# Strassen pairs of column blocks in the last FFN's second matrix, an eighth Strassen block in its first two, and six adaLN sums moved into FoX's head steps

## The reference

```python
for i in range(DEPTH):                       # DEPTH = 2
    mod = c_act @ ada_w[i] + ada_b[i]
    sh_a, sc_a, g_a, sh_f, sc_f, g_f = [m[:, None, :] for m in jnp.split(mod, 6, axis=-1)]
    h = x * (1.0 + sc_a) + sh_a
    y = _mla(h, ...) if i % 2 == 0 else _fox(h, ...)
    x = _layer_norm(ALPHA * x + (1.0 + g_a) * y, ln1_g[i], ln1_b[i])
    h = x * (1.0 + sc_f) + sh_f
    y = (silu(h @ w1) * (h @ w3)) @ w2
    x = _layer_norm(ALPHA * x + (1.0 + g_f) * y, ln2_g[i], ln2_b[i])
```

## Time and profile before

| | |
|---|---|
| median of 3 runs | 2184.3 us (2183.52 to 2187.05) |
| profiled execution | 2183.23 us |
| its span, first to last instruction | 2181.5 us |
| mean granted TensorE clock | 0.997 |
| busy | PE 98%, DVE 77%, ACT 47%, POOL 5% |

### The profile page before, as it was taken

How to read it: one execution, slowest core, us unless ns; L and a number is a source line. 1 busy time by engine, 2 the same in 40 slices (tenths; PEclk the granted TensorE clock), 3 DMA queues, 4 the chain that set the end, 5 groups by cost and what they waited for, 6 DMA issues and landing times.

```text
span 2181.5 us, 25010 instructions
## 1 busy us (share of the span) xinstructions
PE 2130.8 (98%) x9515; PEld 1737.1 (80%) x9515; DVE 1677.3 (77%) x1868; ACT 1024.9 (47%) x1334; POOL 105.1 (5%) x208
## 2 busy tenths in 40 slices
PE   5799999999999999999999999999999999999999
PEld 2378877888888888888788888878888888888887
DVE  6789989787777777778887566878787755787766
ACT  1077636544443444443544454554445534465543
POOL 2101100000000000000000000000000000000000
PEclk9999999999999999999999999999999999999999
DMA  9999997789998898999678778958985765576672
GB/s 388 418 363 365 360 391 271 283 296 336 338 338 328 322 337 323 325 332 366 216 270 329 258 270 288 343 178 267 348 301 206 277 230 175 162 257 217 223 281 85
DMA packets 177065, 635.90 MB, mean 291 GB/s; under 512 B 20385, under 2 KB 51377, under 8 KB 150705
## 3 DMA queue, kind: packets, MB, share of 16 engines
q1 hardware_dynamic: 147298, 427.93, 54.6%
q0 software_dynamic: 27792, 201.34, 24.7%
q10 hardware_dynamic: 1856, 5.04, 0.6%
HBM read 616.37 MB, written 17.86 MB: 291 GB/s over the span
## 4 chain that ended last, share of the span: by engine, by line
PE 87%; DVE 6%; DMA 5%; ACT 1%; issue 1%; POOL 0%; ACTq 0%; SPq 0%; DVEq 0%; POOLq 0%
PE ps L2106 45%; PE ps L2112 22%; PE ps L2409 7%; PE ps L2415 3%; PE ps L2123 3%; DMA gate<-in_ada_w 3%; PE ps L2391 2%; DMA raw<-in_mla_w_o 1%; DVE wlo L1356 1%; PE ps L2396 1%; DMA ada_head<-in_ada_w 1%; DVE ada_w L1393 1%; DVE gate L1393 1%; DMA ada_w<-in_ada_w 1%; PE ps L2335 0%
## 5 line engine op out<-in xcount | busy, mean ns | idle before, releaser
L850 ACT ACTIVATE whi<-raw 128x1024 fp32r<-128x1024 f32 (+1 forms) x645 | 679.0, 1056 | 852.6 <-PE ps L2112 698.4
L1356 DVE TENSOR_TENSOR wlo<-raw,whi 128x1024 fp32r<-128x1024 f32 (+1 forms) x645 | 777.2, 1214 | 356.2 <-ACT whi L850 354.2
L2106 PE MATMUL ps<-whi,hT_hi 128*128 128x512 f32 x1432 | 447.8, 394 | 2.3 <-DVE hT_lo L1784 2.3
L2106 PE MATMUL ps<-whi,hT_lo 128*128 128x512 f32 x1432 | 441.7, 390 | 0.0
L2112 PE MATMUL ps<-wlo,hT_hi 128*128 128x512 f32 x1432 | 382.9, 389 | 0.0
L1393 DVE CUSTOM_DVE_ANT_0 ada_w<-ada_w,c_bc,cols 128x2048 f32<-128x2048 f32 x145 | 339.7, 2344 | 14.8 <-ACT c_bc L1224 8.5
L2106 PEld LDWEIGHTS ps<-whi,hT_lo 128*128 128x128 f32 x1432 | 268.8, 188 | 56.6
L2112 PEld LDWEIGHTS ps<-wlo,hT_hi 128*128 128x128 f32 x1432 | 268.8, 188 | 56.2
L2106 PEld LDWEIGHTS ps<-whi,hT_hi 128*128 128x128 f32 x1432 | 266.1, 188 | 56.1 <-DVE hT_lo L1784 2.9
L2106 PE MATMUL ps<-whi,uT_lo 128*128 128x512 f32 x656 | 201.9, 389 | 0.0
L2106 PE MATMUL ps<-whi,uT_hi 128*128 128x512 f32 x656 | 201.9, 389 | 0.0
(11 more groups left out here) (317 smaller groups left out, 2028.9 us busy)
## 6 DMA issues: line engine op xcount, KB each, us to landing
raw<-in_ffn_w SPq DMA_DIRECT2D x436, 512.0 KB, 5.6
ada_w<-in_ada_w POOLq DMA_DIRECT2D x145, 1024.0 KB, 8.1
raw<-in_fox_w_in SPq DMA_DIRECT2D x96, 512.0 KB, 5.3
raw_more<-in_ffn_w SPq DMA_DIRECT2D x92, 512.0 KB, 5.3
ada_head<-in_ada_w POOLq DMA_DIRECT2D x16, 1024.0 KB, 20.1
raw<-in_mla_w_o SPq DMA_DIRECT2D x32, 512.0 KB, 8.7
raw<-in_fox_w_o SPq DMA_DIRECT2D x32, 512.0 KB, 5.4
gate<-in_ada_w POOLq DMA_DIRECT2D x12, 1024.0 KB, 8.9
```

The costliest lines, as they stand in the source:

```text
L850: nc.scalar.activation(split_hi(pl.unit)[:, 0:n], raw_of(pl.unit)[:, 0:n], ACT.Copy).then_inc(hi_ready, 1)
L1356: nc.vector.tensor_tensor(split_lo(pl.unit)[:, 0:n], raw_of(pl.unit)[:, 0:n], split_hi(pl.unit)[:, 0:n].bitcast(F32), ALU.subtract).then_i ...
L2106: nc.tensor.matmul(ps[:, 2 * pair + t, 0:width], a[:, t * P:(t + 1) * P], w_hi, start=(first and c == 0 and a is hi), stop=False)
```

## The change

Three things:

- `FAST_FROM` goes from 4 to 3: block 3 of the last FFN becomes a Strassen block too, the mixtures are made one block earlier, in block 2.
- In the last FFN's `w2`, pairs of column blocks become Strassen products (`FAST_PAIRS`): both pairs of the first pass and the first pair of the second. Of a pair's 24 (20) units four are replaced by seven operand units of 6 matmuls. The left-hand mixtures are made once per pass from `uT` (`pair_mix_inputs`, `pair_mix_low`, one ACT copy); per pair there are four operand sums, four ACT copies, two corrections, and for each side an addition to the banks' content, the gate's multiplication and the addition to x (`add_pair_side`), which take the place of `residual`.
- Layer 1's last 16 sums need no longer wait for the FFN: `one_ada` names the even steps, and the bound is the end of the list. Six sums leave the last FFN for the second place of FoX's steps 0, 4, 8, 12, 16 and 18.

```diff
-FAST_FROM = 4
+FAST_FROM = 3
...
+FAST_PAIRS = (2, 1)
+PAIR_LEFT, PAIR_RIGHT = (4, 0, 4), (6, 6, 6)
+
+
+def pair_units(n):
+
+    count = 4 * FF_PASSES[n] // UC
+    left, right = ([(side, j) for j in range(2, count)] for side in ("left", "right"))
+    return (left[:-2] + [("B11", 0), ("B21", 1)] + left[-2:] + right[:1] + [("B22", 1), ("T1", 0)]
+            + right[1:3] + [("T2", 0)] + right[3:5] + [("T3", 0)] + right[5:7] + [("T4", 0)] + right[7:])
...
-    return i % 4 == 2 and i < H
+    return i % 2 == 0
...
+    pair_left = [silu_all, place_at("pair_left_1", [P, T, NB], F32, b0 + 20 * KB)]
+    pair_right = [u, place_at("pair_right_1", [P, T, NB], F32, b0 + 44 * KB)]
...
+            def load_pair(n, first, pair, at):
+
+                for kind, j in PAIR_UNITS[n]:
+                    if kind in ONTO:
+                        pl.unit += 1
+                        at += 1
+                        continue
+                    load_down(1, n, first, 2 * pair + (kind in ("right", "B22")), j, at)
+                    at += 1
+                    if kind == "B21":
+                        s, free, _ = BESIDE[pl.unit - 1]
+                        sp.wait_ge(lo_ready, free)
+                        sp.dma_start(raw_tile(s), A["ffn_w2"][1, (2 * pair + 1) * (D_FF // P // UC) + 4 * first // UC]
+                                     ).then_inc(raw_in[s], 16)
+                return at
...
+                if i == FF_PASSES[0]:
+                    act.wait_ge(pair_added, 2 * FAST_PAIRS[0])
...
+            def fast_pair(n, pair, done):
+
+                q, at = n * FAST_PAIRS[0] + pair, PAIR_AT[n]
+                left, right = pair_left[n], pair_right[n]
+                if pair == 0:
+                    units(MIX_AT)
+                    act.wait_ge(mix_summed, 2 + n)
+                    nc.scalar.activation(pair_s_hi[n][:, :, :, :], pair_s_32[n][:, :, :, :], ACT.Copy
+                                         ).then_inc(mix_high, 1)
+                    done += MIX_AT
+                units(at["B11"] + 2 - done)
+                act.wait_ge(units_used, pl.pe - 2)
+                act.wait_ge(pair_added, 2 * q)
+                nc.scalar.activation(left[:, 0, :], ps[:, CHAIN, :], ACT.Copy).then_inc(pair_first_copied, 1)
+                units(at["T1"] + 1 - at["B11"] - 2)
+                act.wait_ge(units_used, pl.pe - 1)
...
-                    if layer == 0 or pl.ada < ada_end(1, SH_F):
+                    if layer == 0 or pl.ada < len(ADA_ORDER):
...
-                    if layer == 0 and i < TICKS - 1 and i not in (0, 2, 4) or layer == 1 and one_ada(i) and pl.ada < ada_end(1, SH_F):
+                    if layer == 0 and i < TICKS - 1 and i not in (0, 2, 4) or layer == 1 and one_ada(i) and pl.ada < len(ADA_ORDER):
...
+            def pair_mix_inputs(n):
+
+                dve.wait_ge(u_low_ready, U_BLOCKS + n * FF_PASSES[0] + 1)
+                dve.wait_ge(units_used, pl.pe)
+                chain(nc.vector.tensor_tensor(pair_mix32[n][:, :, :], uT_hi[:, 0:2 * UC, :].bitcast(F32),
+                                              uT_lo[:, 0:2 * UC, :].bitcast(F32), ALU.add))
+                (a11, a21), (a12, a22) = ([pair_mix32[n][:, x * UC:(x + 1) * UC, t * P:(t + 1) * P]
+                                           for t in range(T)] for x in range(2))
+                s = [pair_s_32[n][:, k, :, :] for k in range(4)]
+                mark(nc.vector.tensor_tensor(s[S1], a21, a22, ALU.subtract))
+                mark(nc.vector.tensor_tensor(s[S3], a11, a21, ALU.subtract))
+                own()
+                chain(nc.vector.tensor_tensor(s[S2], s[S1], a11, ALU.subtract))
+                nc.vector.tensor_tensor(s[S4], s[S2], a12, ALU.add).then_inc(mix_summed, 1)
+
+            def pair_mix_low(n):
+
+                dve.wait_ge(mix_high, 2 + n)
+                nc.vector.tensor_tensor(pair_s_lo[n][:, :, :, :], pair_s_32[n][:, :, :, :],
+                                        pair_s_hi[n][:, :, :, :].bitcast(F32), ALU.subtract).then_inc(mix_ready, 1)
+
+            def add_pair_side(side, bank, read, q, col, last, added):
+
+                dve.wait_ge(units_used, pl.pe)
+                own()
+                nc.vector.tensor_tensor(side[:, :, :], side[:, :, :], ps[:, bank:bank + T, :], ALU.add
+                                        ).then_inc(read, 1)
+                dve.wait_ge(gate_copied, 16 * pl.gate)
+                dve.wait_ge(read, q + 1)
+                for t in range(T):
+                    mark(nc.vector.tensor_tensor(side[:, t, :], side[:, t, :],
+                                                 gate[:, col * NB:(col + 1) * NB], ALU.mult))
+                own()
+                x = xa[:, :, col * NB:(col + 1) * NB]
+                nc.vector.tensor_tensor(x, x, side[:, :, :], ALU.add).then_inc(pair_added, 1)
+                if last:
+                    dve.wait_ge(pair_added, added)
+                    for t in range(T):
+                        mark(nc.vector.bn_stats(stats[:, t, col * 6:(col + 1) * 6],
+                                                xa[:, t, col * NB:(col + 1) * NB]))
+
+            def fast_pair(n, pair, done):
+
+                q, at = n * FAST_PAIRS[0] + pair, PAIR_AT[n]
+                left, right = pair_left[n], pair_right[n]
+                last = n == len(FF_PASSES) - 1
+                if pair == 0:
+                    units(1)
+                    pair_mix_inputs(n)
+                    units(MIX_AT)
+                    pair_mix_low(n)
+                    done += 1 + MIX_AT
+                units(at["T3"] + 1 - done)
+                dve.wait_ge(pair_fifth_copied, q + 1)
+                dve.wait_ge(pair_second_copied, q + 1)
+                dve.wait_ge(pair_third_copied, q + 1)
+                mark(nc.vector.tensor_tensor(right[:, 0, :], right[:, 1, :], right[:, 0, :], ALU.subtract))
+                mark(nc.vector.tensor_tensor(right[:, 1, :], right[:, 1, :], left[:, 1, :], ALU.subtract))
+                units(at["T4"] - at["T3"] - 1)
+                add_pair_side(left, PAIR_LEFT[q], pair_left_read, q, 2 * pair, last, 2 * q + 1)
+                units(len(PAIR_UNITS[n]) - at["T4"])
+                add_pair_side(right, PAIR_RIGHT[q], pair_right_read, q, 2 * pair + 1, last, 2 * q + 2)
...
+                for kind, j in PAIR_UNITS[n]:
+                    if (kind, j) == ("left", 2) and pair == 0:
+                        pe.wait_ge(u_low_ready, made - 1)
+                    if (kind, j) == ("left", count - 2) and pair == 0:
+                        pe.wait_ge(u_low_ready, made)
+                    if (kind, j) == ("left", 2) and pair == 0 and n == 1:
+                        pe.wait_ge(pair_left_read, q)
+                    if (kind, j) == ("right", 2):
+                        pe.wait_ge(right_read, done)
+                        if q:
+                            pe.wait_ge(pair_right_read, q)
+                    if kind == "B11":
+                        if q:
+                            pe.wait_ge(pair_third_copied, q)
+                        operand(CHAIN, rows_of_u(0, 0), True, True)
+                    if kind == "T1":
+                        if q:
+                            pe.wait_ge(pair_fifth_copied, q)
+                        operand(FIFTH, mixed_u(S1), True, True)
+                    if kind == "T2":
+                        pe.wait_ge(pair_first_copied, q + 1)
+                        operand(CHAIN, mixed_u(S2), False, True, True)
+                    if kind == "T3":
+                        pe.wait_ge(pair_second_copied, q + 1)
+                        operand(CHAIN, mixed_u(S3), False, True, True)
+                    if kind == "B21":
+                        operand(left, rows_of_u(1, 0), False, False)
+                    if kind == "T4":
+                        operand(left + 1, rows_of_u(1, 1), False, True)
+                    if kind == "B22":
+                        pe.wait_ge(mix_ready, 2 + n)
+                        operand(right, mixed_u(S4), False, False)
+                    if kind == "left":
+                        plain(left, j, j == 2, (j == count - 1, False))
+                    if kind == "right":
+                        plain(right, j, j == 2, (j == count - 1, j == count - 1))
...
```

141 lines of the change are left out of this document (114 added, 27 removed).

## The result

The changed kernel takes 2189.8 us (median of 20 runs, 2186.2 to 2192.7), the kernel before 2185.2 us (20 runs beside it). The ratio is 1.0019 with an interval of 1.0013 to 1.0025: about 4 us slower (the medians are 4.6 us apart), just inside what I had called no change, and 0.2 us above my range. I had started from 2184.3 us, the median of 3 runs of the kernel before; 20 runs put it at 2185.2, so 0.9 us of the distance to my 2184.2 is the starting point, and the rest is the change.

The account below looks back on a forecast made before the run. PE was taken as the bound, busy 2130.8 of 2181.5 us. Removed matmuls (-5.4) plus a stall in FoX's last steps (+5.3) gave -0.1 us, forecast 2184.2 us, 8-in-10 range 2178.6 to 2189.6.

Parts of the forecast that it names:

- what the change takes away: Last FFN: 24 fewer matmuls on PE at 0.227 us each, 5.4 us saved, with nothing overlapping.
- block 3 and the pairs cost nothing off PE: Last FFN: the added DVE and ACT work makes PE wait nowhere; priced at nothing.
- the pairs are not free: Rival, last FFN: PE waits 1 to 2 us in each of three pairs, time 2187 to 2190 us; 7%.
- the place: FoX's last steps: PE waits for the low half near 1403 to 1412 us, DVE's sums for DMA in steps 17 and 18.
- the stall doesn't come: Rival, FoX's last steps: loads are quick, PE loses less than 1 us, time 2178.9 us; 20%.
- the size of the stall: FoX's last steps: PE stands still for 5.3 us, with bounds of 1.7 and 8.1 us.
- With 7.3: the sum of step 17 can start at 1399.0.: FoX's last steps: with the median load time of 7.3 us, step 17's sum starts at 1399.0 and ends at 1401.3.
- My upper bound: FoX's last steps: with loads of 8.7 us the low half ends at 1414.4, a stall of 8.1 us.
- Where I began to follow the buffers: FoX's step 16, with times of the earlier trace; its added sum's data, issued at 1384.34, arrive at most 8.7 us later.
- In two pieces of 0.9 and 4.4.: Stall split: 0.9 us at P times V of head 15, 4.4 at the unit needing head 15's low half.
- The lower bound, 1.7: FoX's last steps: with loads of 5.0 us only the sums are in the way, leaving 1.7 us of stall.
- The rival of the clock: Rival, FoX's last steps: PE's clock falls after the stall, adding up to 3.3 us; 2190.3 us with 8.7 us loads; 15%.

Follow-up runs that it names:

- sums_early: Changed kernel with the six moved sums in FoX's steps 0, 1, 4, 5, 8 and 9 instead of 0, 4, 8, 12, 16 and 18: 2177.9 us.
- only_18: Changed kernel with the second sums of steps 12 and 16 moved to steps 5 and 9, step 18's kept: 2185.0 us.
- only_12: Changed kernel with the second sums of steps 16 and 18 moved to steps 5 and 9, step 12's kept: 2179.3 us.
- look_2: The changed kernel itself, nothing altered, one more profiled execution: 2189.4 us.
- not_18: Changed kernel with step 18's second sum moved to step 9, the other five kept: 2184.1 us.
- sums_alone: Kernel before with the six sums moved as in the changed kernel, without Strassen block 3 and pairs: 2194.2 us.

## Why the prediction was wrong

**Right: what the change takes away.** 24 x 0.227 = 5.4 us; measured 5.4 to 5.5 in each of the five executions and in the variants with both parts.

**Right: block 3 and the pairs cost nothing off PE.** The windows came out at 42.16, 63.92 twice and 53.04 us, and PE waits for nothing in the last FFN. A side's work on DVE in the second pass is 1.22 + 1.29 + 1.23 + 1.29 = 5.0 us by its timeline, as worked out. The rival *the pairs are not free* did not come.

**Right in kind: the place.** Waits for low halves between 1400 and 1415 us, with sums of steps 17 and 18 that wait for DMA. The rival *the stall doesn't come* is out.

**Wrong: the size of the stall, 5.3 us with bounds of 1.7 and 8.1.** This is the term of the sum that failed: the head steps measured +7.5 in the profiled execution and 6.8 to 15.2 over five, 9.5 on average. The other term, -5.4, came as forecast. Three things in that step failed.

- *"With 7.3: the sum of step 17 can start at 1399.0."* I took the median of loads that ran about one a step. With the chain full they took 8.7 at the median and up to 8.8, in two other executions up to 10.4. My upper bound was the longest of eight landings in a chain with slack, and with the change the loads are longer: three more of them come in these steps. The medians from 1362 to 1405 us are 5.6 to 7.3 us in the seven executions without a second sum in step 12 (before, sums_early and only_18 among them), and 7.1 to 9.0 in the ten that have it and full loads. A bound read from before's landings bounds nothing there.
- *Where I began to follow the buffers.* I started at step 16 with before's times (1384.34 for an issue). But the sum added in step 12 had already used up the lead: sums of steps 14, 15 and 16 wait 0.97, 1.75 and 1.28 us for DMA, and the load that I had at 1384.34 is issued only behind the late sum of step 15, at 1388.21. In only_18, which has no second sum in step 12, those of 14 and 15 wait for nothing. By itself the lost lead costs nothing (only_12).
- *"In two pieces of 0.9 and 4.4."* It was 1.1, 2.8 and 1.3 in the profiled execution; how it is divided varies, and look_2 with 0.5 and 6.5 has my two places. I saw step 18's sum as the cause; not_18 shows that without it 6.3 of 7.5 us stay, only_18 that alone it costs 4.4. They don't add up because both hold the same chain; either is enough to use up a slack of 0.5 us. The lower bound, 1.7, was also too low: with quick loads it was 3.2.

**The rival of the clock came, in part.** Its time with loads of 8.7 us, 2190.3, is nearest to the result, and loads of 8.7 did come, but that it is so near is luck: it adds 3.3 us of clock that the profiled execution did not pay, and its stall of 8.1 was exceeded in two of the five. The clock fell in the head steps of all five executions, but it adds to the time only where no wait is left behind it. I had added 3.3 us on top of the stall; in the profiled execution it added nothing, in only_18 1.8. By the Trainium skill ("TensorE: Matmul & The Clock Gate", part 1) the array is throttled unless activity releases it. The traces agree in direction, 0.67 in the window above and 0.50 to 0.60 behind longer waits, but not in each case: behind the 2.83 us of sums_alone it is 1.00.

**Open.** Why the loads land at 8.7 us in one execution and 10.4 in the next is not shown. Nor is why the wait near 980 us is frequent in the changed kernel (its code there is the same), nor what else makes the part ahead of the head steps longer.

## What to carry to other kernels

Work that waits for a load should go where a step is long against the buffer's cycle: here load + work + issue is 11.4 us for a buffer, 5.7 per item with two buffers. Steps of 6.5 us hold one item, six-unit steps two, and the same six sums cost 7 to 15 us or nothing depending on where they stand. When following such a chain, start at the first step that gets an extra item, not at the one where it hurts, and give the loads a longer time than the trace of the lighter kernel shows: here 8.7 and up to 10.4 us instead of 7.3. And the version to keep is the one that takes the gain without the stall: 2177.9 us.
